# Own buffers for 16 modulation tiles of the merge stage, one addition for each gate bias, and row operations moved away from rotations

## What is computed

```python
s_lat, s_ctx = silu(c), silu(c_ctx)
for l in range(2):
    shift, scale, gate = split(s_lat @ w_mod[l] + b_mod[l], 3)          # w_mod[l]: 2048 x 6144
    shift_c, scale_c, gate_c = split(s_ctx @ w_mod[l] + b_mod[l], 3)
    hx = rmsnorm(x, norm_g[l]) * (1 + scale) + shift
    hc = rmsnorm(ctx, norm_g[l]) * (1 + scale_c) + shift_c
    ...
    ctx = ctx + gate_c * y_c                                            # not in the last layer
    x = x + gate * y
return rmsnorm(x, final_g)
```

## Time and profile before

| | |
|---|---|
| median of three executions | 2537.25 us |
| profiled execution | 2542.52 us |
| its span | 2540.7 us |
| TensorE busy (matmuls) | 2493.9 us, 98% |
| VectorE busy | 2062.5 us, 81% |
| ScalarE busy | 1267.6 us, 50% |
| GpSimd busy | 101.7 us, 4% |
| mean DMA rate | 224 GB/s |
| mean granted TensorE clock | 0.995 of full |

### The profile page before, as it was taken

How to read it: one execution, slowest core, us unless ns; L and a number is a source line. 1 busy time by engine, 2 the same in 40 slices (tenths; PEclk the granted TensorE clock), 3 DMA queues, 4 the chain that set the end, 5 groups by cost and what they waited for, 6 DMA issues and landing times.

```text
span 2540.7 us, 30618 instructions
## 1 busy us (share of the span) xinstructions
PE 2493.9 (98%) x11754; PEld 2047.6 (81%) x11754; DVE 2062.5 (81%) x2635; ACT 1267.6 (50%) x1754; POOL 101.7 (4%) x151
## 2 busy tenths in 40 slices
PE   8999999999999898999999999999999999999998
PEld 6888888878888676788888888888888888888887
DVE  6998898888898777866998867898875885888866
ACT  6545544544543333455445654446555454455654
POOL 0000000000000000000200000020000000200000
PEclk9999999999999999999999999999999999999999
DMA  9777576677777666787665567954446777544454
GB/s 353 253 249 250 194 263 236 217 237 239 231 256 256 242 226 232 272 269 266 211 207 184 183 229 252 326 173 148 152 149 248 283 257 240 183 150 149 149 190 174
DMA packets 350866, 570.22 MB, mean 224 GB/s; under 512 B 18369, under 2 KB 203073, under 8 KB 346881
## 3 DMA queue, kind: packets, MB, share of 16 engines
q1 hardware_dynamic: 343216, 532.87, 61.7%
q0 software_dynamic: 6784, 34.65, 3.8%
q10 hardware_dynamic: 720, 0.75, 0.1%
HBM read 559.79 MB, written 8.41 MB: 224 GB/s over the span
## 4 chain that ended last, share of the span: by engine, by line
PE 79%; DVE 9%; DMA 6%; issue 3%; ACT 2%; SPq 0%; POOL 0%; DVEq 0%; ACTq 0%
PE acc L586 23%; PE acc L588 23%; PE acc L587 23%; DVE w_lo L574 3%; PE aux L1239 2%; DMA raw<-in_w_in 1%; PE aux L1264 1%; ACT w_hi L566 1%; DMA raw<-in_w_mod 1%; DMA raw<-in_w_rnn_out 1%; DVE cacc L2512 1%; DMA raw<-in_w_o 1%; PE aux L1387 1%; DVE rows_z L2171 1%; PE aux L1249 1%
## 5 line engine op out<-in xcount | busy, mean ns | idle before, releaser
L566 ACT ACTIVATE w_hi<-raw 128x1024 fp32r<-128x1024 f32 x808 | 843.5, 1058 | 881.8 <-PE acc L588 638.7
L574 DVE TENSOR_TENSOR w_lo<-raw,w_hi 128x1024 fp32r<-128x1024 f32 x808 | 990.4, 1229 | 333.7 <-ACT w_hi L566 332.5
L586 PE MATMUL acc<-w_hi,h_hi 128*128 128x512 f32 x2240 | 894.2, 399 | 22.6 <-DVE w_lo L574 22.5
L588 PE MATMUL acc<-w_hi,h_lo 128*128 128x512 f32 x2240 | 876.5, 391 | 0.0
L587 PE MATMUL acc<-w_lo,h_hi 128*128 128x512 f32 x2240 | 875.7, 391 | 0.0
L586 PEld LDWEIGHTS acc<-w_hi,h_hi 128*128 128x128 f32 x2240 | 422.9, 189 | 124.2 <-DVE w_lo L574 22.4
L588 PEld LDWEIGHTS acc<-w_hi,h_lo 128*128 128x128 f32 x2240 | 422.4, 189 | 90.7
L587 PEld LDWEIGHTS acc<-w_lo,h_hi 128*128 128x128 f32 x2240 | 423.0, 189 | 83.8
L586 PE MATMUL acc<-w_hi,u_hi 128*128 128x512 f32 x800 | 320.3, 400 | 4.9 <-DVE w_lo L574 4.5
L588 PE MATMUL acc<-w_hi,u_lo 128*128 128x512 f32 x800 | 313.2, 391 | 0.0
L587 PE MATMUL acc<-w_lo,u_hi 128*128 128x512 f32 x800 | 313.0, 391 | 0.0
(11 more groups left out here) (374 smaller groups left out, 2141.9 us busy)
## 6 DMA issues: line engine op xcount, KB each, us to landing
raw<-in_w_in SPq DMA_DIRECT2D x631, 512.0 KB, 4.7
raw<-in_w_mod SPq DMA_DIRECT2D x104, 512.0 KB, 5.8
raw<-in_w_out SPq DMA_DIRECT2D x96, 512.0 KB, 4.8
rows_in<-in_w_mod SPq DMA_DIRECT2D x88, 512.0 KB, 6.3
raw<-in_w_rnn_out SPq DMA_DIRECT2D x32, 512.0 KB, 6.3
raw<-in_w_o SPq DMA_DIRECT2D x32, 512.0 KB, 6.5
raw<-in_w_attn_out SPq DMA_DIRECT2D x16, 512.0 KB, 5.6
xr_s<-x_mid POOLq DMA_DIRECT2D x4, 1024.0 KB, 12.5
```

The source lines that it names most:

```text
L566: act.activation(w_hi[:, n % NSPLIT], raw[:, slot, (n % 2) * SK:(n % 2) * SK + SK], ACT.Copy).then_inc(hi_ready, 1)
L574: dve.tensor_tensor(w_lo[:, n % NSPLIT], raw[:, slot, (n % 2) * SK:(n % 2) * SK + SK], w_hi[:, n % NSPLIT].bitcast(F32), ALU.subtract).the ...
L586: pe.matmul(acc[pair][m][:, :], a_hi[:, k0 + k, tok], w_hi[:, s, k], start=b, stop=False)
L588: last = pe.matmul(acc[pair][m][:, :], a_lo[:, k0 + k, tok], w_hi[:, s, k], start=False, stop=e)
```

## The change

It does six things.

1. `HALVES`: 16 of the 24 tiles of halves 6, 7 and 8 get own slots (0 to 2); the other eight (tiles 0 and 1 of half 6, tile 6 of half 7, tiles 0, 2, 4, 6 and 7 of half 8) stay in the ring. Slots 0 and 2 share one semaphore, slot 1 has the other.
2. The places of the row operations in halves 2 to 8 are new. None stands any more at granules 50 to 52 of iterations 1 and 2. Half 8 ends at granule 117 of the merge stage instead of 111.
3. The planner takes from `CLEAR` or from `own_before` when a buffer comes free, for all own tiles.
4. `load_own` has new waits for halves 6 to 8; ScalarE's wait ahead of `m_hi` in chunks 1 and 3 and VectorE's ahead of half 8 are now on row operations that read the buffers there.
5. `gaterows` of layer 0 lie elsewhere, both in the same place; `gate_bias` fills the buffer with zeros first, and starts later; GpSimd waits for the writes of the first gate before it fills for the second.
6. `gate_add` is one addition over the partitions 0 to 96 (or 0 to 32) instead of 4 (or 2) of one partition.

```diff
     Half(0, 1, 0, 2, (0, None) * 4, tiles_at((SG1, (
-        33, 34, 35, 36, 42, 43, 44, 45, 46, 46, 48, 49, 50, 50, 53, 53, 54, 55)), (2 * SG1, (
+        33, 34, 35, 36, 42, 43, 44, 45, 46, 46, 48, 49, 53, 53, 54, 54, 55, 55)), (2 * SG1, (
...
     Half(0, 1, 1, 2, None, tiles_at((2 * SG1, (
-        14, 14, 15, 16, 17, 17, 18, 18, 21, 23, 23, 24, 30, 31, 32, 33, 34, 35, 35, 36, 44, 46, 46, 47, 50, 50, 51, 53, 53, 54, 54, 55)))),
+        14, 14, 15, 16, 17, 17, 18, 18, 21, 23, 23, 24, 30, 31, 32, 33, 34, 35, 35, 36, 44, 46, 46, 47, 53, 53, 54, 54, 55, 55,
+        56, 56)))),
     Half(1, 0, 0, 2, None, tiles_at((3 * SG1, (
-        2, 3, 4, 5, 5, 6, 6, 7, 10, 12, 12, 13, 13, 14, 14, 15, 17, 17, 18, 18, 20, 20, 21, 23, 24, 24, 25, 27, 31, 33, 34, 34)))),
-    Half(1, 0, 1, 2, None, tiles_at((3 * SG1, (45, 46, 46, 47, 48, 48, 49, 50, 53, 53, 54, 55)), (S2, (
-        1, 1, 2, 4, 5, 5, 6, 7, 10, 10, 11, 12, 12, 13, 14, 14, 15, 15, 16, 17)))),
-    Half(0, 2, 0, 2, None, tiles_at((S2, (
-        17, 18, 18, 19, 20, 20, 21, 23, 24, 25, 26, 27, 29, 30, 31, 32, 34, 35, 36, 37, 38, 38, 39, 40, 41, 42, 43, 44, 45, 46, 48, 48)))),
-    Half(0, 2, 1, 2, None, tiles_at((S2, (
-        49, 50, 51, 52, 52, 53, 54, 55, 57, 58, 59, 60, 62, 63, 64, 65, 65, 66, 67, 68, 69, 70, 71, 72, 73, 73, 75, 76, 77, 78, 79, 80)))),
-    Half(1, 1, 0, 2, None, tiles_at((S2, (
-        81, 82, 83, 83, 85, 86, 88, 88, 90, 91, 92, 93, 94, 95, 96, 97, 97, 98, 99, 100, 102, 103, 104, 105, 106, 107, 107, 108, 109, 109, 110,
-        111)))),
+        2, 4, 4, 5, 7, 7, 8, 10, 12, 12, 13, 13, 14, 14, 15, 16, 17, 17, 18, 19, 20, 20, 23, 23, 30, 31, 32, 33, 34, 35, 35, 36)))),
+    Half(1, 0, 1, 2, None, tiles_at((3 * SG1, (
+        45, 46, 46, 47, 48, 48, 49, 50, 53, 53, 54, 55)), (S2, (
+        0, 0, 1, 4, 5, 5, 6, 7, 10, 10, 11, 12, 13, 17, 17, 18, 18, 19, 19, 20)))),
+    Half(0, 2, 0, 2, (None, None, 1, 0, 1, 0, 1, 0), tiles_at((S2, (
+        20, 21, 22, 23, 24, 25, 26, 27, 27, 28, 30, 32, 32, 33, 35, 36, 37, 38, 39, 40, 41, 41, 42, 43, 44, 45, 46, 48, 49, 50,
+        51, 52)))),
+    Half(0, 2, 1, 2, (1, 0, 1, 2, 1, 2, None, 2), tiles_at((S2, (
+        52, 53, 53, 55, 56, 57, 59, 60, 61, 62, 64, 65, 65, 66, 67, 68, 69, 70, 71, 72, 73, 73, 75, 76, 77, 78, 79, 80, 81, 82,
+        83, 83)))),
+    Half(1, 1, 0, 2, (None, 2, None, 2, None, 2, None, None), tiles_at((S2, (
+        85, 87, 88, 89, 90, 92, 93, 94, 94, 95, 96, 97, 98, 99, 100, 101, 102, 103, 104, 105, 106, 107, 108, 108, 109, 110, 111,
+        112, 113, 115, 116, 117)))),
...
-FIRST_CLEAR = {0: 12, 1: AT[0][-1], 2: AT[1][-5], 9: S4 + 9, 10: X0 - 2, 11: C1 - 8}
+CLEAR = {(0, 0): 12, (0, 1): 12, (1, 0): AT[0][-1], (1, 1): AT[0][-1], (2, 0): AT[1][-5], (6, 2): S2 + 18, (6, 3): S2 + 20, (7, 0): AT[6][-5],
+         (7, 1): AT[6][-1], (7, 3): AT[6][-1] + 2, (8, 1): AT[7][-1], (9, 0): S4 + 9, (9, 1): S4 + 9, (10, 0): X0 - 2, (10, 1): X0 - 2,
+         (11, 0): C1 - 8, (11, 1): C1 - 8}
...
+            before = own_before(("half", h, t))
+            clear = CLEAR[h, t] if (h, t) in CLEAR else AT[h][2 * x.values * (before + 1) - 1]
             start = min(max(first - 6, clear + 6), first)
...
+                ((rt + 4 * KB, rt + 20 * KB), (rt + 32 * KB, rt + 48 * KB), (rt + 12 * KB, rt + 28 * KB)),
...
+            elif h == 7 and i == 3:
+                sp.wait_ge(mod_sums, 7)
             if own_before(item) is not None:
 
                 sp.wait_ge(mod_rows, rows_after(h, own_before(item)))
...
+            elif h == 6 and i == 2:
+                sp.wait_ge(pv_ps, 2 * IT1)
+                sp.wait_ge(roped, 4 * NG * IT1)
+            elif h == 6:
+                sp.wait_ge(mod_sums, 6)
+            elif h == 7:
+                sp.wait_ge(mod_rows, rows_after(6, HALF_TILES - 2 + i))
+            elif h == 8:
+                sp.wait_ge(mod_rows, rows_after(7, HALF_TILES - 1))
...
             def gate_bias(l, i, half, values):
+                pool.memset(gaterows[i][:, :], 0.0).then_inc(gate_zero, 1)
+                pool.wait_ge(gate_zero, i + 1)
...
-            pool.wait_ge(roped, 4 * NG * IT1)
+            pool.wait_ge(oT_lo, IT1)
             gate_bias(0, 0, 0, 2)
-            pool.wait_ge(oT_lo, IT1)
...
-            pool.wait_ge(mod_sums, 7)
+            pool.wait_ge(gate_out, 16 * 4)
             gate_bias(0, 1, 1, 2)
             gate_rows(0, 1, 1, 2)
+            pool.wait_ge(gate_out, 16 * 8)
...
-                            if chunk == NCH - 1:
-                                act.wait_ge(gate_out, 16 * 8)
+                            if chunk != 2:
+                                act.wait_ge(mod_rows, rows_after(7, 1) if chunk == 1 else rows_after(8, 5))
...
-                        dve.wait_ge(gate_out, 16 * 4)
+                        dve.wait_ge(mod_rows, rows_after(7, 4))
...
-                for j in range(strips):
-                    r = slice(32 * j, 32 * j + 1)
-                    i = dve.tensor_tensor(gaterows[g][r, :], X[3][r, :], gaterows[g][r, :], ALU.add)
-                    step.link(i) if j < strips - 1 else i.then_inc(mod_chunk, 1)
+                r = slice(0, 32 * strips - 31)
+                dve.tensor_tensor(gaterows[g][r, :], X[3][r, :], gaterows[g][r, :], ALU.add).then_inc(mod_chunk, 1)
```

More of the change, by code:

```diff
@@ L175, in own_queue, with own_before @@
     return None if own_slot(item) is None else own_slot(item) % 2
+def own_before(item):
+    _, h, i = item
+    return max([t for t in range(i) if own_queue(("half", h, t)) == own_queue(item)], default=None)
 LOADS, taken = [], 0
 BEFORE_PAIR = [[] for _ in range(GRANULES // 2 + 1)]
-FIRST_CLEAR = {0: 12, 1: AT[0][-1], 2: AT[1][-5], 9: S4 + 9, 10: X0 - 2, 11: C1 - 8}
+CLEAR = {(0, 0): 12, (0, 1): 12, (1, 0): AT[0][-1], (1, 1): AT[0][-1], (2, 0): AT[1][-5], (6, 2): S2 + 18, (6, 3): S2 + 20, (7, 0): AT[6][-5],
+         (7, 1): AT[6][-1], (7, 3): AT[6][-1] + 2, (8, 1): AT[7][-1], (9, 0): S4 + 9, (9, 1): S4 + 9, (10, 0): X0 - 2, (10, 1): X0 - 2,
+         (11, 0): C1 - 8, (11, 1): C1 - 8}
 for h, x in enumerate(HALVES):
@@ L185 @@
         if own_slot(("half", h, t)) is not None:
-            clear = FIRST_CLEAR[h]
-            if t >= 2:
-                clear = AT[h][2 * x.values * (max(t - 2, 6 * (h == 11 and t == 7), 5 * (h == 9 and t == 6)) + 1) - 1]
+            before = own_before(("half", h, t))
+            clear = CLEAR[h, t] if (h, t) in CLEAR else AT[h][2 * x.values * (before + 1) - 1]
             start = min(max(first - 6, clear + 6), first)
@@ L198 @@
 OWN = [item for item in LOADS if item not in PLACE]
-def own_before(item):
-    _, h, i = item
-    return max([t for t in range(i) if own_queue(("half", h, t)) == own_queue(item)], default=None)
 def own_uses(item):
@@ L326, in build_program @@
         bns = at("bns", cm + 4352, [P, NT, 6])
-        gaterows = [at(f"gaterows{i}", a, [P, CH]) for i, a in enumerate((o3 + 26 * KB, rt + 28 * KB, regU + 28 * KB, regH + 14 * KB))]
+        gaterows = [at(f"gaterows{i}", a, [P, CH]) for i, a in enumerate((cm + 2048, cm + 2048, regU + 28 * KB, regH + 14 * KB))]
         rows_u = [at(f"rows_u{v}", regU + 12 * KB + 16 * KB * v, [P, HALF]) for v in range(2)]
@@ L337, in build_program @@
         ones = small[:, 40:41]
-        slots_p1, slots_c0, slots_x0, slots_c1 = [
+        slots_p1, slots_p2, slots_c0, slots_x0, slots_c1 = [
             [[at(f"rows_in{i}{a}{j}", off, [P, 2, CH]) for j, off in enumerate(pair or ())] for a, pair in enumerate(pairs_at)]
@@ L345, in build_program @@
                 ((regO + 8 * KB, regO + 12 * KB), (regO, regO + 4 * KB), None, (rt + 46 * KB, rt + 50 * KB))))]
-        own = {0: slots_p1, 1: slots_p1, 2: slots_p1, 9: slots_c0, 10: slots_x0, 11: slots_c1}
+        own = {0: slots_p1, 1: slots_p1, 2: slots_p1, 6: slots_p2, 7: slots_p2, 8: slots_p2, 9: slots_c0, 10: slots_x0, 11: slots_c1}
         kc = at("kc", regO, [P, H2, T])
@@ L441, in build_program @@
         mod_rows, mod_sums, rows_in = sem("mod_rows"), sem("mod_sums"), [sem(f"rows_in{i}") for i in range(2)]
-        mod_zero, tables_in, gate_out = sem("mod_zero"), sem("tables_in"), sem("gate_out")
+        mod_zero, gate_zero, tables_in, gate_out = (sem(n) for n in ("mod_zero", "gate_zero", "tables_in", "gate_out"))
         MOD = uses("mod", dict(wdw_in=16, small_in=96, lam_p=1, lam_e=1), LAYERS)
```

## The result

The kernel after took 2505.28 us, median of 4 runs (2503.11 to 2506.43), and the kernel before 2536.99 us beside it: ratio 0.987, 95% interval 0.986 to 0.989, or 31.7 us less. The forecast was 36 less. The profiled execution took 2506.43 us with a span of 2504.4. Against the profiled execution of before (2542.5) that is 36.1 us less, so the trace went as far as the forecast said, and the median 4.3 us less far.

What follows compares the result with a forecast made beforehand. Prediction: SyncE's ring of four slots has no slack in the merge stage's second half, so TensorE waits on w_lo. Terms -29 - 8 + 1 = -36 us, taken from the median 2537.25, give 2501 us; range 2489 to 2520.

Steps and rivals of the forecast that it cites:

- The stretch and its floor: Second half of the merge stage, 828.5 to 1061.1 us: 197.5 us without loss, so 35 of 232.6 us are loss.
- (a): Merge stage, halves 6 to 8: own buffers for 16 of 24 tiles end most of the ring's stall, saving 29 us.
- The 6 us that were to stay: Merge-stage loss left despite own buffers: 4.5 us for half 8's last two tiles, 1.5 us for first starts.
- (b): SyncE's queue: new waits of own tiles cost nothing while TensorE's distance holds, up to 3 us if not.
- The tile named as the worst: Half 7's tile 3: SyncE waits from granule 57 to granule 60's row operation, three granules, before its load.
- The sign that I had named for being wrong: SyncE's waits for own tiles coming to over 7 us each would show the prediction wrong.
- The rival "slower": Own tiles block SyncE's queue, fourteen waits of 12 us: 2574 us; slower from about 9.5 us. Chance 0.06.
- (c): VectorE in the stretch: 93% busy against 197.5 us, keeps up; by the DRAIN rule 5 us more loss left.
- (d): Gate bias: twelve additions become four, 5.5 us less VectorE work, load to 90%, nothing counted beside the path.
- (e): Row operations moved off rotations in iterations 1 and 2 and the probabilities' turning: saves 8 us, bounds 4 and 9.
- (f): End of merge stage: half 8 ends six granules later, so source(0) loads later; 1 us lost, bounds 0 and 6.
- more loss than (f) behind the stretch: Sign of being wrong: rows near 1090 to 1120 us losing more than the 1 us priced for the later source(0).

Runs made afterwards that it cites:

- e2: Kernel after with all tiles of halves 6, 7 and 8 back in the ring, at the new places: 2552.72 us, ratio 1.0055.
- e4: Kernel after with own slots kept, but row operations of halves 5 to 8 at the places of before: 2500.69 us, ratio 0.9844.
- e5: Kernel before with the gate part alone (one addition over 97 or 33 partitions, moved and zero-filled gaterows, later waits): 2534.84 us, ratio 0.9982.
- e6: Kernel before with GpSimd's source(0) load held until granule 119 of the merge stage: 2540.0 us, ratio 1.0003.
- e0: Kernel before, run again unchanged: 2538.05 us.
- e3: Kernel before with only the new row-operation places of halves 2 and 3, away from the rotations: 2532.28 us, ratio 0.997.

## Why the prediction was right, and where it was not

**The stretch and its floor** were right: 197.5 us forecast for 71 granules without loss, 197.3 measured.

**(a) Own buffers**: the mechanism was right and is shown (e2 undoes it alone), the size was low: 35.3 us saved where the step said 29. 35.3 is nearly all slots: with the old places 198.6 us are reached too (e4). The 6 us that were to stay, 4.5 for half 8's last two ring tiles and 1.5 for first starts, aren't in the stretch. The ring tiles did cost something, but behind the stretch, where I hadn't looked.

**(b) SyncE's waits** at no cost: right, with little to spare. The tile named as the worst, half 7's tile 3, is the worst, but it holds the queue 16.7 us, not three granules (8 us). The step counted granules at TensorE's pace. It left out that VectorE, on whose row operation SyncE waits, stands still at an evacuation on the way, 3.95 us for TensorE's accumulator. Timelines of SyncE, VectorE and ScalarE in the kernel after:

```profile
855.41 18.34 SPq L550 DMA_DIRECT2D rows_in<-in_w_mod  x4
...
862.79 0.69 DVE L2353 TENSOR_TENSOR mt<-sig,acc 128x512 f32<-128x512 f32 x1 [3.95 <-PE acc L605]
...
881.18 2.01 ACT L583 ACTIVATE w_hi<-raw 128x1024 fp32r<-128x1024 f32 x2 [3.57 <-DMA raw<-in_w_rnn_out]
```

ScalarE then waits 3.57 us for the pair, and TensorE none. But of its distance, from the end of `w_lo` to the first matmul with it 6.5 us at granule 57, the evacuation and this wait leave 1.4 to 2.2 us at granules 62 to 68. The sign that I had named for being wrong (over 7 us for an own tile) came, once, and cost nothing. What fourteen such waits would cost, no run shows. The rival "slower" is refuted all the same: all waits of own tiles from 820 us on come to 31 us in 9 waits, not to fourteen of 9.5 or more.

**(c) VectorE's load** fell from 182.70 of 232.6 us to 174.74 of 197.3, 89%, where 90 were forecast. `w_lo` and the row operation still start 1.14 and 1.19 us after one another while each takes 1.22 and 1.28. By the rule of the Trainium skill (VectorE: DVE Perf Modes, The DRAIN you can't avoid), taken as the full duration for each operation, 5 us more of loss would have stayed. None did, so neither the starts nor the stretch bear out that reading of it here; the same section of the Trainium skill says that an operation which is not held starts earlier, and the prediction left that out.

**(d) The gate part** beside the path, at nothing: this step failed. The four additions take 0.677 us each, as forecast (0.685), and the fills 0.53. But "VectorE is not the bound" doesn't mean that its work is free. With the gate part alone the kernel before gained 4.6 us (e5), 2.4 to 3.5 of them probably in the ring's stretch. That they come over slots which VectorE frees earlier fits the ring waits (74.5 us for `rows_y` there, 77.7 to 78.9 in e6, e0 and before), and is argued, not shown. Within the whole change nothing can be added for it: at the floor there is no stall left for it to shorten.

**(e) Rotations**: 1.2 + 6.3 + 1.9 - 0.9 = 8.5 us against 8, each term near its own (0.99, 6.3, 1.70 and 1). The cause named for the 1 us lost was wrong. I put it on half 3's doubled operations, but e3, which has these, takes the 174.4 us of before for granules -56 to 0. e4, with the new places of half 4 and the old ones behind, takes 175.1, and e2, with the new places and no own slots, 175.3. So most of it is left to half 4's places, though no run changes these alone.

**(f) The later `source(0)`**: this is the term that was mis-sized, 1 us (bounds 0 to 6) against 9.1. The step followed one load to one reader, ScalarE's squares, and that reader was indeed hardly late: it waited 1.46 us. It left out that half 8's last ring tile holds SyncE's queue up to the same granule, and that the 3 MB behind `source(0)` then meet pairs which have no distance left. The prediction had named more loss than (f) behind the stretch as a sign of being wrong, and it came.

**The sum**: the errors cancel, and that is luck. By the table of stretches (a) brought 6.3 us more than forecast, (e) 0.5 more, the rest of the span 1.6, and (f) lost 8.1 more: -36.3 between the two spans against -36. The 4 us by which the forecast missed the median fit the step that took the gain of the profiled execution off the median of others. That execution was 5.3 us above it, and e0 shows a difference of 5.5 us in the very stalls that the change removes. Where the removed loss is what varies, the gain off the median is smaller: 36 - 5.3 = 30.7 us, and 31.7 was measured. The range of 2490 to 2508 us was said to follow from the bounds of (a) to (f), and does not: together these give 2493 to 2525.

## What to carry to other kernels

A queue that issues in order and shares a ring between two users is bounded by slot time, from issue over landing to the last reader, against one turn of the ring; own slots for the slow user gave 34 of the 35 us here (e4). When work moves out of a stall to a later place, look at what starts there: one tile read out of the ring just ahead of one burst of loads cost 9 us, and with either moved away the loss was gone. Before an executed profile's gain is taken off a median, ask whether the surplus of that execution sits in the part being removed.

## What the runs showed of the hardware that was not expected

A stall varies between executions where steady work doesn't. In the four traces with the ring and the old additions (before, e0, e3, e6) granules 41 to 112 took 228.8 to 232.6 us, and in the four with the old places at the rotation of iteration 2 (before, e0, e5, e6) its six granules took 22.1 to 25.3 us, while granules -112 to -62, without a stall, took 154.1 us in all twelve traces. And when GpSimd's queue and SyncE's carried transfers at once, at up to 453 GB/s in a slice of the DMA view of the kernel after, a 512 KB transfer took 26.98 us from issue to landing, where the median of all 631 loads of `in_w_in` is 4.7. TensorE feels that only where the loads aren't far enough ahead: in the kernel before such transfers took 15.7 us at the median, and the eight granules lost nothing.
